# Expert stage of a mixture-of-experts layer: late loads moved behind the weights, empty places left out of the token gathers and of the result's stores, the whole result scratch cleared in front

## The reference, cut to what matters

```python
TOP_K = 2; N_EXPERTS = 32; D_EXPERT = D_MODEL // 2          # D_MODEL = 1024
# each token picks 2 experts; tokens are sorted by expert and cut into blocks
def expert_block(args):
    xe, e = args
    hid = jax.nn.silu(xe @ w_gate[e]) * (xe @ w_up[e])
    return hid @ w_down[e]
yb = lax.map(expert_block, (xb, blk_e)).reshape(-1, D)
contrib = yb[slot] * gate_s[:, None].astype(h.dtype)
return jnp.zeros_like(h).at[tok_s].add(contrib)
```

## Time and profile before

| | us |
|---|---|
| median of 3 runs | 1092.08 |
| lowest and highest | 1088.38, 1095.23 |
| the profiled execution's own time | 1088.47 |
| its span, first to last instruction | 1086.7 |
| PE busy | 1013.6 (93%) |
| DVE busy | 689.5 (63%) |
| ACT busy | 457.5 (42%) |
| POOL busy | 387.9 (36%) |

### The profile page before, as it was taken

How to read it: one execution, slowest core, us unless ns; L and a number is a source line. 1 busy time by engine, 2 the same in 40 slices (tenths; PEclk the granted TensorE clock), 3 DMA queues, 4 the chain that set the end, 5 groups by cost and what they waited for, 6 DMA issues and landing times.

```text
span 1086.7 us, 17545 instructions
## 1 busy us (share of the span) xinstructions
PE 1013.6 (93%) x4944; PEld 615.6 (57%) x4945; DVE 689.5 (63%) x1151; ACT 457.5 (42%) x585; POOL 387.9 (36%) x416
## 2 busy tenths in 40 slices
PE   5999996998999997999999999799999899799996
PEld 5899985886888752444444344233344344258885
DVE  6588999888223273557557556456655557567886
ACT  6445446666223123345335336225434525343332
POOL 2168775688000303233333232232332323023310
PEclk9999997899999988999999999899999999999999
DMA  9221962212123499999999999999999999956531
GB/s 280 70 59 40 259 183 78 75 50 78 59 97 142 191 410 380 416 346 368 419 417 419 417 420 416 417 419 417 418 417 418 419 417 420 413 186 213 177 133 44
DMA packets 90402, 299.26 MB, mean 275 GB/s; under 512 B 10737, under 2 KB 41489, under 8 KB 65788
## 3 DMA queue, kind: packets, MB, share of 16 engines
q1 hardware_dynamic: 75227, 263.63, 62.2%
q0 software_dynamic: 7296, 22.29, 5.7%
q10 hardware_dynamic: 7840, 12.85, 3.2%
HBM read 261.20 MB, written 37.54 MB: 275 GB/s over the span
## 4 chain that ended last, share of the span: by engine, by line
PE 47%; DMA 8%; DVE 4%; issue 3%; SPq 1%; DVEq 1%; ACT 1%; POOL 0%; POOLq 0%; ACTq 0%
PE ps_gate_up L2150 25%; PE ps_y L2162 12%; DMA raw_weights<-w_exp_up 7%; PE ps_gate L72 3%; PE ps_gate L70 3%; PE ps_gate L71 3%; DVE h_turned L2090 1%; PE ps_proj L1721 1%; PE ps_h3t L2449 1%; DVE weights L114 1%; DVE x_turned L2080 1%; DMA late_room<-y_rows,out_rows 1%; SPq L92 0%; DVEq L1938 0%; DMA x_tokens<-h_rows,item_tokens 0%
## 5 line engine op out<-in xcount | busy, mean ns | idle before, releaser
L2150 PE MATMUL ps_gate_up<-weights,x_turned 128*64 128x512 f32 x1568 | 354.7, 604 | 22.5 <-DVE x_turned L2080 22.0
L2150 PEld LDWEIGHTS ps_gate_up<-weights,x_turned 128*64 128x64 f32 x1568 | 131.9, 140 | 236.5 <-issue 232.4
L114 ACT COPY weights<-raw_weights 128x2048 f32 x93 | 174.9, 1900 | 163.6 <-PE ps_gate_up L2150 78.9
L2162 PE MATMUL ps_y<-weights,h_turned 128*64 128x512 f32 x784 | 177.7, 593 | 2.6 <-DVE h_turned L2090 2.6
L114 DVE COPY weights<-raw_weights 128x2048 f32 x93 | 114.3, 1229 | 84.6 <-DMA raw_weights<-w_exp_up 52.5
L463 POOL TENSOR_TENSOR conv_pool_taps<-conv_pool_taps,tap_product 128x448 f32<-128x448 f32 (+1 forms) x88 | 135.9, 1544 | 39.5 <-ACT tap_product L569 29.3
L1995 POOL COPY x_tokens<-x_tokens_next 128x512 f32<-128x512 f32 x48 | 37.5, 782 | 286.8 <-DMA x_tokens_next<-h_rows,token_ids 201.1
L2090 DVE STREAM_TRANSPOSE h_turned<-hidden 32x128 f32<-32x128 f32 x392 | 118.6, 303 | 33.1 <-PE ps_y L2162 27.6
L127 POOL DMA_INDIRECT x_tokens_next<-h_rows,token_ids x96 | 112.5, 1172 | 52.9 <-POOL token_ids L122 38.3
L2162 PEld LDWEIGHTS ps_y<-weights,h_turned 128*64 128x64 f32 x784 | 65.3, 137 | 105.7 <-issue 101.9
L914 DVE SCALAR_TENSOR_TENSOR taps_bank<-a_ext,par,taps_bank 128x640 f32<-128x640 f32 (+1 forms) x128 | 101.5, 793 | 3.3
(11 more groups left out here) (293 smaller groups left out, 1470.6 us busy)
## 6 DMA issues: line engine op xcount, KB each, us to landing
raw_weights<-w_exp_gate SPq DMA_DIRECT2D x62, 1024.0 KB, 14.5
raw_weights<-w_exp_up SPq DMA_DIRECT2D x62, 1024.0 KB, 16.4
raw_weights<-w_exp_down SPq DMA_DIRECT2D x62, 1024.0 KB, 14.4
y_rows<-y_tile ACTq DMA_DIRECT2D x96, 128.0 KB
y_rows<-zero_rows SPq DMA_DIRECT2D x16, 512.0 KB, 6.2
x_rows<-x_tile SPq DMA_DIRECT2D x9, 512.0 KB, 2.6
h_rows<-h_tile SPq DMA_DIRECT2D x9, 512.0 KB, 2.9
late_room<-x_rows SPq DMA_DIRECT2D x9, 512.0 KB, 4.6
```

What stands on the lines that cost most here:

```text
L114: copy(S.work[s][:, :], raw).then_inc(S.w_ready[s], 1)
L2150: last = pe.matmul(ps_gu[side[j], :, :], x_t[:, k, :], w[:, :, c, share(D_EXP, j)], start=(k == 0), stop=(k == KD - 1))
L2162: last = pe.matmul(ps_y[side[j], :], h_t[:, k, :], w[:, share(D, j)], start=(k == 0), stop=(k == KE - 1))
```

## The change

The token numbers of empty places get a value far out of range (`EMPTY`, 8192), and the gathers are told to leave out numbers beyond the bound. A second list, `y_ids`, holds for each item and partition the half row of `y_rows` that it belongs to, or a number out of range where the place is empty. It takes one more product on PE, two more small steps on DVE ahead of `item_tokens` and a cast behind it. POOL, not ACT, stores an item's result: one indirect DMA that scatters 128 half rows of 2 KB and leaves the empty ones out, three items late (`LAG`). The last item alone is stored by ACT as before. Since rows of empty places are no longer written, all of `y_rows` is cleared in front: 32 pieces of 128 rows and a half piece, where it was 16 and a half. On SP `late_ple_proj` goes behind the last expert's pieces, and the three gain rows behind `w_ple_gate`. Three small tiles of the tail share another buffer.

```diff
+EMPTY = 1 << 13
+LAG = 3
...
     for g in range(TURNS):
         pool.indirect_dma_start(out=rows[:, g, :], out_offset=None,
                                 in_=S.h2_rows.rearrange("t (q n) -> (t q) n", q=QUARTERS),
-                                in_offset=bass.IndirectOffsetOnAxis(ap=ids[g], axis=0)).then_inc(landed or S.x_gathered, 16)
+                                in_offset=bass.IndirectOffsetOnAxis(ap=ids[g], axis=0),
+                                bounds_check=QUARTERS * ROWS - 1, oob_is_err=False).then_inc(landed or S.x_gathered, 16)
...
-                with sp.Fori(EXPERTS * BLOCK // P, ITEMS * BLOCK // P) as e:
+                with sp.Fori(0, ITEMS * BLOCK // P) as e:
                     sp.dma_start(S.y_rows[bass.ds(e * P, P), :].rearrange("p (j n) -> p j n", n=P),
                                  S.zero[:, :].unsqueeze(1).to_broadcast([P, KD, P])).then_inc(S.y_cleared, 16)
...
                 for g in range(TURNS):
-                    last = pe.matmul(ps_ids[:, g, :], quarters[0:BLOCK, g, :], item_list[:, :], start=True, stop=True)
-                last.then_inc(placed, 1)
+                    pe.matmul(ps_ids[:, g, :], quarters[0:BLOCK, g, :], item_list[:, :], start=True, stop=True)
+                pe.matmul(ps_ids[:, TURNS, :], S.x_tokens[0:BLOCK, 0, P:], item_list[:, :], start=True, stop=True).then_inc(placed, 1)
...
                 dve.wait_ge(placed, 3)
-                ts(tokens_low[:, :, :], ps_ids, tab.own_quarter[:, :], None, ALU.add)
+                ts(tokens_low[:, :, :], ps_ids[:, 0:TURNS, :], tab.own_quarter[:, :], None, ALU.add)
+                dve.wait_ge(quarters_set, 2)
+                ts(y_low, ps_ids[:, TURNS, :], -0.5, float(2 * EMPTY), ALU.is_gt, ALU.mult)
+                stt(y_low, y_low, y_side, y_base, ALU.subtract, ALU.add)
                 step(dve.tensor_copy(S.item_tokens[:, :, :], tokens_low[:, :, :]))
                 dve.sem_inc(S.tokens_ready, 1)
+                step(dve.tensor_copy(S.y_ids[:, :], y_low))
...
                 for s in PIECES:
                     load_piece(sp, S, s, 2, 1, slice(2, 3))
-                sp.dma_start(S.late_w[:, :, :], ple_proj).then_inc(S.proj_w_loaded, 16)
...
-                half = FIXED + (EXPERTS - FIXED) // 4 * 2
-                with sp.Fori(FIXED, half, 2) as n:
-                    for odd in range(2):
-                        load_set(n + odd, odd)
-                for rows, src, loaded in zip((S.g_ple_rows, S.b_ple_rows, S.g_final_rows), gains,
-                                             (S.g_ple_loaded, S.ple_rows_loaded, S.ple_rows_loaded)):
-                    sp.dma_start(rows[:, :], src.partition_broadcast(P)).then_inc(loaded, 16)
-                with sp.Fori(half, EXPERTS - 1, 2) as n:
+                with sp.Fori(FIXED, EXPERTS - 1, 2) as n:
                     for odd in range(2):
                         load_set(n + odd, odd)
                 load_set(EXPERTS - 1, 0)
+                sp.dma_start(S.late_w[:, :, :], ple_proj).then_inc(S.proj_w_loaded, 16)
...
+                for rows, src, loaded in zip((S.g_ple_rows, S.b_ple_rows, S.g_final_rows), gains,
+                                             (S.g_ple_loaded, S.ple_rows_loaded, S.ple_rows_loaded)):
+                    sp.dma_start(rows[:, :], src.partition_broadcast(P)).then_inc(loaded, 16)
                 for s in DOWN:
                     sp.wait_ge(w_ready[s], EXPERTS - 1)
...
+                def scatter(i, behind, of=y):
+                    ids = S.ids[:, TURNS:] if of is y else S.ids[:, 0:1]
+                    more = LAG - behind
+                    pool.wait_ge(y_left, i + more + 2)
+                    pool.sem_inc(S.waits_met, 1)
+                    pool.tensor_copy(ids, S.y_ids[:, bass.ds(i - behind, 1)]).then_inc(y_id_ready, 1)
+                    pool.wait_ge(y_id_ready, i + more + 1)
+                    pool.sem_inc(S.waits_met, 1)
+                    pool.indirect_dma_start(out=S.y_rows.rearrange("t (h n) -> (t h) n", h=SIDES),
+                                            out_offset=bass.IndirectOffsetOnAxis(ap=ids, axis=0), in_=of[:, :], in_offset=None,
+                                            bounds_check=SIDES * BLOCK * ITEMS - 1, oob_is_err=False).then_inc(y_scattered, 16)
...
+                with pool.Fori(LAG, n_last) as i:
+                    move(i)
+                    gather(i + 1)
+                    scatter(i, LAG)
                 move(n_last)
+                scatter(n_last, LAG)
+                scatter(n_last, LAG - 1)
+                scatter(n_last, 1, y_end)
                 pool.wait_ge(S.ple_split, 4)
-                pool.wait_ge(y_stored, n_last * 16 * SIDES + 32 * SIDES)
+                pool.wait_ge(y_scattered, n_last * 16)
+                pool.wait_ge(y_stored, 16 * SIDES)
...
                 def leave_y(i, to=y):
                     act.wait_ge(w_used[USED_AT[DOWN[1]]], i + 1)
-                    if to is y:
-                        act.wait_ge(y_stored, i * 16 * SIDES + 16 * SIDES)
+                    if to is y and not (type(i) is int and i == 0):
+                        act.wait_ge(y_scattered, i * 16)
                     act.activation(to[:, :], ps_y[:, :], ACT.Copy).then_inc(y_left, 1)
...
-                        leave_y(i - 1)
-                        if not final:
-                            store_y(i - 1)
-                    if final:
-                        store_y(i - 1)
+                        leave_y(i - 1, y_end if final else y)
```

More of the change, by code:

```diff
@@ L59 @@
 FIXED = 3
+EMPTY = 1 << 13
+LAG = 3
+assert EMPTY > BLOCK * ITEMS
+assert EMPTY > QUARTERS * ROWS
 assert FIXED == QUARTERS - 1
@@ L1562, in routing_tables @@
         quarter = QUARTERS - 1 - e
-        pool.affine_select(out=t.own_quarter[:, :], in_=t.own_quarter[:, :], compare_op=ALU.is_ge, fill=float(quarter - 1),
+        pool.affine_select(out=t.own_quarter[:, :], in_=t.own_quarter[:, :], compare_op=ALU.is_ge, fill=float(EMPTY + quarter - 1),
                            base=-quarter * QUAD, pattern=[[0, 1]], channel_multiplier=1)
@@ L1659, in _ @@
                 for g in range(TURNS):
-                    copied = pool.tensor_copy(quarters[:, g, :].rearrange("p (q b) -> p q b", b=QUAD),
+                    pool.tensor_copy(quarters[:, g, :].rearrange("p (q b) -> p q b", b=QUAD),
                                               S.ident[:, g * QUAD:(g + 1) * QUAD].unsqueeze(1).to_broadcast([P, QUARTERS, QUAD]))
-                copied.then_inc(quarters_set, 1)
+                sides = S.x_tokens[:, 0, P:].rearrange("p (j b) -> p j b", b=BLOCK)
+                pool.tensor_copy(sides, S.ident[:, 0:BLOCK].unsqueeze(1).to_broadcast([P, SIDES, BLOCK]))
+                pool.iota(y_base, pattern=[[BLOCK * SIDES, ITEMS]], base=0, channel_multiplier=SIDES, allow_small_or_imprecise_dtypes=True)
+                pool.memset(y_side, float(P - 1))
+                pool.memset(S.x_tokens[:, 1, P + ITEMS + 1:], 0.0).then_inc(quarters_set, 1)
+                pool.wait_ge(quarters_set, 1)
+                pool.affine_select(out=y_side, in_=y_side, compare_op=ALU.is_ge, fill=0.0,
+                                   base=-BLOCK, pattern=[[0, 1]], channel_multiplier=1).then_inc(quarters_set, 1)
                 pool.wait_ge(S.h2_stored[0], 16 * ((T + 1) // 2))
+                pool.wait_ge(quarters_set, 2)
                 pool.wait_ge(S.tokens_ready, 1)
@@ L1925, in experts @@
         h_t = sb("h_turned", [P, KE, BLOCK])
-        y, y_end = sb("y_tile", [P, D // SIDES]), sb("y_tile_end", [P, D // SIDES])
+        y, y_end, y_last = (sb(n, [P, D // SIDES]) for n in ("y_tile", "y_tile_end", "y_tile_last"))
         psum = lambda n, s: ctx.enter_context(nc.psum_tensor(n, s, F32))
@@ L1995, in move @@
                     pool.tensor_copy(x[:, :, :], x_next[:, :, :]).then_inc(x_moved, 1)
+                def scatter(i, behind, of=y):
[9 more added lines that the diff above has]
+                                            bounds_check=SIDES * BLOCK * ITEMS - 1, oob_is_err=False).then_inc(y_scattered, 16)
+                pool.memset(x_next[:, :, :], 0.0).then_inc(x_cleared, 1)
+                pool.wait_ge(x_cleared, 1)
                 gather(1)
-                with pool.Fori(1, n_last) as i:
+                pool.sem_inc(y_id_ready, LAG)
+                for i in range(1, LAG):
                     move(i)
                     gather(i + 1)
+                with pool.Fori(LAG, n_last) as i:
+                    move(i)
+                    gather(i + 1)
+                    scatter(i, LAG)
                 move(n_last)
+                scatter(n_last, LAG)
+                scatter(n_last, LAG - 1)
+                scatter(n_last, 1, y_end)
                 pool.wait_ge(S.ple_split, 4)
-                pool.wait_ge(y_stored, n_last * 16 * SIDES + 32 * SIDES)
+                pool.wait_ge(y_scattered, n_last * 16)
+                pool.wait_ge(y_stored, 16 * SIDES)
                 pool.sem_inc(S.waits_met, 1)
@@ L2049, in gate_hi @@
```

(12 more changed lines are left out.)

24 lines of the change are left out of this document (14 added, 10 removed).

## The result

The changed kernel takes 1096.11 us (median of 6, 1093.28 to 1099.00), the kernel before beside it 1089.79 us (median of 6). The ratio is 1.005, 95% interval 1.0029 to 1.0071: half a per cent slower, where the prediction had it 1.2% faster (1077 us, range 1066 to 1091). The profiled execution has a span of 1094.8 us, 8.1 more than before.

The account below looks back on a forecast made before the run. In the expert stage PE and the DMA engines were taken to share the bound, with PE losing 21.2 us to stops for weights. The profiled 1088.5 - 19 (stage) + 6 (front) + 1 (routing) gave 1076.5, so 1077 us, range 1066 to 1091.

Parts of the forecast that it names:

- The front, +6: Ahead of the experts: 16 added clears delay w_out and the norm behind it, +6 us, bounds +2 to +10.
- The rival that clears cost nothing: In front: by the skill's line rate w_out arrives before ACT asks, no loss, 1070.5 us; chance 0.08.
- The routing, +1: End of the routing: one more PE product and two more DVE steps before the first gather, +1 us (0.5 to 1.5).
- That empty rows cost no transfer: Expert stage: if empty rows cost no transfer, 20.6 us of gather and store DMA time go.
- That rival: Expert stage: empty rows still cost their transfer, only the late loads leave, 1090.5 us; chance 0.10.
- The end, nothing: Tail: late_ple_proj pushes w_ple_gate back 2.5 us and the gains follow, costed at nothing; +2 if cover is gone.
- The stage, -19: Expert stage: less DMA traffic removes most of PE's 21.2 us of stalls, -19 us, bounds -21.2 and -12.
- My balance of 82.0 us of supply against 82.4 of demand: One run of 8 items in the expert stage: 34.3 MB of DMA need 82.0 us against PE's 82.4.
- The rival of the late scatter: Expert stage: ACT's leave waits for the previous item's scatter; 1107 us at a landing of 10.8 us; chance 0.09.
- my own sign: Expert stage: if ACT's wait before y_tile passes 7 us, the scatter is the new wait.
- my limits of 8.1 and 9.8 us: Scatter landing in the expert stage: above 8.1 us ACT's weight copy is late, above about 9.8 us PE stops.
- The floor I gave ACT's copy, 504.92: One expert round: ACT's next duty after the leave is the weight copy at 504.92, so landings at 502.6 or 503.5 go unnoticed.

Follow-up runs that it names:

- The run of that alone: Kernel before, with only the empty places left out of the token gathers; results stored by ACT as before: 1085.07 us, ratio 0.9945.
- two tiles: Changed kernel with two y tiles alternating by item, so ACT's leave of item k waits for the scatter of item k-2: 1091.98 us, ratio to before 1.0010.
- the best kernel: Changed kernel with two y tiles, 16 clears spread over the first seven token tiles, late_ple_proj and gains at the stage's start: 1081.43 us, ratio to before 0.9926.
- its five variants: Changed kernel with half the clears moved (1089.03 us), late loads back (1092.25), only gains back (1093.68), two y tiles (1091.98), or everything placed (1081.43).
- the three without a scatter: Kernel before with gathers without empty places (1085.07 us), gains at the stage's start (1087.10), or both (1082.38).
- the two parts without a scatter: Kernel before with empty places left out of the gathers and the three gain loads at the start of the expert stage: 1082.38 us, ratio 0.9923.

## Why the prediction was wrong

The forecast was 1076.5 from -19 + 6 + 1, with the end at nothing. The profiled execution gives -8.2 + 6.6 + 1.3 + 8.4 = +8.1.

- **The front, +6: right.** 32 clears, `w_out` issued at 174.64 (said 174.8), ACT released by DMA `w_out_raw` at 185.18 (said 184), +6.6 us. The rival that clears cost nothing is out: the added 16 moved at 270 GB/s, and moving them gave 5.7 to 7.1 us, of which the front's share is 6.2 at the `h_rows` store. The Trainium skill, page "DMA: Bandwidth & Descriptors", section Specifications, gives the line rate for pieces from 512 bytes on; these runs do not show it for these pieces, and the measurement decides.
- **The routing, +1: right**, 1.3.
- **That empty rows cost no transfer: right.** The run of that alone shows a third of the gathers' bytes and time gone. That rival is out. The number of packets did not fall (4416 in both), but 960 of them are left with 16 bytes each, and these take 0.6 us of the 16 engines in all.
- **The end, nothing: wrong.** The step was "The gains follow, 3.8 us, and are used after the first gather of results. I cost both at nothing; if the cover is gone, +2." I asked who uses the gains, and not who stands behind them in the engines: the store of the last result and the first gather. The store landed 2 us later than in the runs without the gains there (4.3 us instead of 2.3), the gather was issued at 958.21 and not at 955.86, PE paused for 5.24 us, and what I had not priced at all, PE came back at the lower clock. With the gains elsewhere the end is 137.1 to 137.3 us long (three runs), and 142.4 to 144.7 with them there (three). So they cost 5 to 8 of the 8.4 us; the last us, 137.2 against 135.5 to 136.2 without a scatter, stays open.
- **The stage, -19: the mechanism was right, the size was not, and this is the largest miss (10.8 us).** The step "I leave 0.4 us of stall in each of some five runs" left 2.2 us of stops; 12.5 were measured, against 21.4 before. Some four of the ten missing us are the scatter's landing in the first rounds, gone with two tiles (8.3 left). The other 6 are in every variant with the scatter: 8.9 in the best kernel, one of 3 to 4 us at the last run of single-item experts, which the kernel before has as well (3.5), and about 1 us at each of the others. There the DMA share is 1.01 and 1.02, so the transfers bound it. My balance of 82.0 us of supply against 82.4 of demand assumed that weights move as fast as before. Beside the scatter they move a little slower: in the traces an 8 KB packet of weights takes 319 to 322 ns on its engine in the changed kernel and its five variants, and 316 to 317 in the kernel before and the three without a scatter. Over the 447 us of such packets 1.2% is some 5 us, an estimate. It doesn't settle the matter: the best kernel has the lowest figure, 319 ns, and no fewer stops, and the two parts without a scatter leave 10.7 us. No run changes the scatter alone, and the cause of these 6 us stays open. Another 1.8 us went in the last item, where PE ran at a granted clock of 0.91 behind a stop of 3.0 us (before 1.00); I had not priced that. The first two items gave 1.2 back. And 2.5 us of the 26.9 were never to be had: with `late_ple_proj` at the start of the stage it is 532.4 us long, with it behind the weights 532.9.
- **The rival of the late scatter: its wait came, and a part of its price.** I had the landing right (6.4 to 7.9 us, median 7.0; said 6.4 to 7.9) and the wait passed 7 us, my own sign. By my limits of 8.1 and 9.8 us nothing should have stopped at such landings. PE stopped all the same, 1.99 us for ACT's copy at 464.43 and 1.02 us behind a late silu at 479.40, because the scatter was itself late in those rounds: ACT was ready to leave at 465.7, and the scatter that it had to wait for was issued at 466.49, behind the two gathers. I had reckoned with one round alone, in which the scatter went 4.8 us before ACT was ready. It was some 4 us and not the 31 per us of landing. ACT's late copies also delay SP's next loads (none between 460 and 477 us), and the DMA engines have gaps; but no later stop is shown to come from that, since from the 19th item on the stops are 8.0 us with one tile and 8.3 with two. The floor I gave ACT's copy, 504.92, held two DMA issues that the change removes, and left out the 1.3 us between a leave and a copy.

The Trainium skill, page "SBUF — State Buffer", section "SBUF: two separate sides", says that GpSimd and a two-port copy on DVE share a pair of ports which each holds for its whole instruction. The trace agrees: next to a DVE copy of weights GpSimd's copy of the row numbers took 1.05 us (at 494.62) instead of 0.18. In the price it did not show: with two y tiles GpSimd did the same work and ACT waited for no scatter.

## What to carry to other kernels

Cost a moved load by what is queued behind it in the DMA engines, and not only by who reads it. Here the same 1.5 MB cost 3 to 5 us in a stretch that transfers bound, 5 to 8 us in front of the hand-over between two stages, and nothing where PE set the pace and the engines still had gaps; look for such a stretch first. Less traffic returns at most the stops that traffic causes, and here about half of them: 8.9 of 21.4 us, and 13.1 once the wait that the change had added (the landing of a scatter before its only tile is free) was gone. Find such a wait in all rounds, not in one, and look at what the clock does behind a stop.

## What the runs showed of the hardware

- An indirect DMA with a bound leaves rows with numbers out of range out of the transfer: 12.06 MB of gathers became 8.00 MB and 4.2% of the engines' time instead of 6.2%, at the same 4416 packets. In the scatter it is so too: gathers and results together fell from 24.12 to 16.59 MB.
- Clears of 512-byte pieces keep all 16 engines busy at 270 to 288 GB/s, where windows of mostly 8 KB packets reach 418.
- A scatter of 128 rows by GpSimd was through 6.4 to 7.9 us after its issue in the changed kernel, where ACT waited for it (median 7.0).
- After 5.3 us with 0.06 us of work PE ran for 6 us at a granted clock of 0.50; where the pause at this place was 0.2 to 0.9 us, it did not. In the stage it came back lower behind a stop of 3.86 us (0.79 over the next 21 us) and behind one of 3.03 (0.91 over 18.7 us), and not behind one of 3.26 us (1.00).
